# Eight gate slabs of a gated linear attention layer, moved into the scan as fp32 products

## The reference

```
p = h @ w_in                      # columns: q (512), k (512), v (1024), g (1024)
log_decay = log_sigmoid(low @ w_a2 + b_a) / 16          # per direction
for both directions, chunk by chunk (state is 128 x 256 for each of 4 heads):
    cum   = cumsum(log_decay)
    attn  = sum_d q[t,d] k[s,d] exp(cum[t,d] - cum[s,d])      # s before t
    out   = attn @ v + (q * exp(cum)) @ state
    state = exp(last) * state + (k * exp(last - cum))^T @ v
y = (rms_norm(out_forward + out_backward) * silu(g)) @ w_out
```

## Time and profile before

| | us |
|---|---|
| median of 3 runs | 1839.11 (1838.51 to 1839.13) |
| profiled execution | 1844.17 |
| its span on the core | 1842.4 |
| TensorE busy | 1687.5 (92%) |
| VectorE busy | 1166.0 (63%) |
| ScalarE busy | 727.2 (39%) |
| GpSimd busy | 110.0 (6%) |

### The profile page before, as it was taken

The page is one execution under the profiler, slowest core; times in us unless marked ns, Lnnn a source line. Parts: engine busy times, 40 slices in busy tenths (PEclk is TensorE's granted clock), DMA queues, the critical chain, the costliest instruction groups (busy, mean ns, idle before and its releaser), DMA issues.

```text
span 1842.4 us, 24024 instructions
## 1 busy us (share of the span) xinstructions
PE 1687.5 (92%) x8912; PEld 1436.4 (78%) x8912; DVE 1166.0 (63%) x1822; ACT 727.2 (39%) x1066; POOL 110.0 (6%) x70
## 2 busy tenths in 40 slices
PE   8999889987999999999997999976679799999996
PEld 6888777876888888888886778865567588888875
DVE  6688566469777577756855652158975665464465
ACT  3212555335342232322334562345533454343334
POOL 0200000123000000000012300000001200000002
PEclk9999999988999999999998899988879799999998
DMA  8334000131334333343221111200012123333221
GB/s 337 118 139 158 26 1 1 51 110 41 120 125 137 106 134 115 114 137 126 80 83 57 35 57 58 79 23 1 1 46 69 46 91 94 100 92 101 92 91 69
DMA packets 37278, 159.48 MB, mean 87 GB/s; under 512 B 4145, under 2 KB 4401, under 8 KB 31057
## 3 DMA queue, kind: packets, MB, share of 16 engines
q1 hardware_dynamic: 37202, 158.44, 25.7%
HBM read 156.33 MB, written 2.10 MB: 86 GB/s over the span
## 4 chain that ended last, share of the span: by engine, by line
PE 80%; DVE 11%; ACT 4%; issue 3%; DMA 1%; POOL 1%; SPq 0%; ACTq 0%; POOLq 0%; DVEq 0%
PE pm L402 63%; PE pm L422 5%; PE pm L594 4%; DVE row L1331 1%; DVE probs L1354 1%; PE pm L443 1%; DMA ada_w<-first_ada 1%; PE pm L717 1%; DVE h_res L1617 1%; ACT probs L878 1%; PE pm L530 1%; PE pm L470 1%; DVE o_r L1622 1%; PE pm L434 1%; PE pm L543 1%
## 5 line engine op out<-in xcount | busy, mean ns | idle before, releaser
L1180 DVE TENSOR_TENSOR w_lo<-raw,w_hi 128x1024 fp32r<-128x1024 f32 x193 | 243.2, 1261 | 425.7 <-ACT w_hi L807 423.4
L402 PE MATMUL pm<-x_hi,w_hi 128*128 128x512 f32 x1600 | 474.1, 356 | 14.0 <-DVE acc_g L1502 9.9
L402 PE MATMUL pm<-x_hi,w_lo 128*128 128x512 f32 x1600 | 473.5, 355 | 0.0
L402 PE MATMUL pm<-x_lo,w_hi 128*128 128x512 f32 x1600 | 470.7, 354 | 0.0
L807 ACT ACTIVATE w_hi<-raw 128x1024 fp32r<-128x1024 f32 x191 | 202.3, 1059 | 671.3 <-PE pm L402 616.0
L402 PEld LDWEIGHTS pm<-x_hi,w_hi 128*128 128x128 f32 x1600 | 262.9, 190 | 64.5 <-issue 15.6
L402 PEld LDWEIGHTS pm<-x_lo,w_hi 128*128 128x128 f32 x1600 | 261.0, 190 | 43.8
L402 PEld LDWEIGHTS pm<-x_hi,w_lo 128*128 128x128 f32 x1600 | 261.7, 190 | 42.8
L402 PE MATMUL pm<-hid_hi,w_hi 128*128 128x512 f32 (+1 forms) x396 | 119.6, 356 | 1.4 <-DVE w_lo L1180 1.4
L402 PE MATMUL pm<-hid_hi,w_lo 128*128 128x512 f32 (+1 forms) x396 | 120.6, 359 | 0.0
L402 PE MATMUL pm<-hid_lo,w_hi 128*128 128x512 f32 (+1 forms) x396 | 119.1, 355 | 0.0
(11 more groups left out here) (200 smaller groups left out, 2405.5 us busy)
## 6 DMA issues: line engine op xcount, KB each, us to landing
raw<-slabs SPq DMA_DIRECT2D x193, 512.0 KB, 3.5
ada_w<-ada SPq DMA_DIRECT2D x44, 1024.0 KB, 4.9
ada_w<-first_ada SPq DMA_DIRECT2D x4, 1024.0 KB, 18.8
h_res<-x SPq DMA_DIRECT2D x4, 768.0 KB, 16.9
out<-h_res SPq DMA_DIRECT2D x8, 256.0 KB, 2.0
rope<-rope SPq DMA_DIRECT2D x1, 512.0 KB, 23.4
level_f<-level SPq DMA_DIRECT2D x1, 448.0 KB, 4.2
vec<-vec SPq DMA_DIRECT2D x1, 272.5 KB, 2.8
```

The costliest lines, as they stand in the source:

```text
L402: last = pe.matmul(out_p[:, a:b], w[slot][:, ks], x[:, k, a:b], start=(k == 0 and w is w_hi and x is hi), stop=(k == tiles - 1 and w is w_lo))
L1180: dve.tensor_tensor(w_lo[nxt % 2][:, :], raw[nxt % 4][:, :], w_hi[nxt % 2][:, :].bitcast(FP32), ALU.subtract).then_inc(sem["split_lo"], 1)
```

## The change

The gate slabs leave the slab sequence (`slabs` has 185 instead of 193) and come as an input of their own, `gates`. They are not split. VectorE adds `x_hi` and `x_lo` back to fp32 for the 512 latent tokens (`join`, eight tiles `x_sum`, in the places of `w_hi` and `w_lo`). TensorE multiplies `gates` by `x_sum` in fp32, one product of 128x512 for each of the 8 x 8 tile pairs; they go in groups of three, three and two ahead of the level product in steps 0 to 23 of the 28. A half bank of `pm[2]` takes them, so the fifth turned key moves to `pm[1]` and the fifth state sum within `pm[2]`. ScalarE copies each gate slab out (`copy_gate`) and takes silu of two slabs once a head, behind the root (`open_gate`). SP loads gates into `raw[1]` and `raw[2]` in turn; the first two before the masks, the others behind them. The first two output slabs are loaded once gate products 7 and 8 are done, and split by ScalarE at b = 4 and VectorE at b = 5 and 6 of the last head, where before that was done in the gate stage. VectorE's masked copy of level b moves from step b to step b+1, behind `level_sides`; ScalarE's block copies likewise, level 6 to the start of the next head behind its first `level_decay`. The value loops of ScalarE and VectorE are unrolled. `sides0`, `sides1` and `o_lo2` change places in the memory of `x_hi` and `x_lo`.

```diff
@@ SP
+            def gate_load(i):
+                if i < 2:
+                    sp.wait_ge(sem["split_lo"], S_GLA_OUT - 3 + i)
+                else:
+                    sp.wait_ge(sem["gate_done"], i - 1)
+                sp.dma_start(gate_raw(i)[:, :], gates_in[i]).then_inc(gate_in[i % 2], 16)
+            gate_load(0)
+            gate_load(1)
             sp.wait_ge(sem["v_copied"], TOK // P + 8)
             sp.dma_start(level_f[:, :, :], level_in).then_inc(sem["level_in"], 16)
-            for u in range(3):
-                slab_load(4 * 29 + u, u)
+            for i in range(2, KT):
+                gate_load(i)
+            for u in range(2):
+                sp.wait_ge(sem["gate_done"], KT - 1 + u)
+                slab_load(S_GLA_OUT + u, 1 + u)
@@ TensorE
-            with pe.Fori(0, 2) as i:
-                for u in range(4):
-                    slab(S_GLA_G, i, u, x_hi, x_lo, LAT)
+            def gate_tiles(step_):
+                i = step_ // 3
+                if i >= KT:
+                    return
+                first = 3 * (step_ % 3)
+                if first == 0:
+                    pe.wait_ge(gate_in[i % 2], 16 * (i // 2 + 1))
+                    if i >= 1:
+                        pe.wait_ge(sem["gate_copied"], i)
+                for k in range(first, min(first + 3, KT)):
+                    pe.wait_ge(sem["x_sum"], k + 1)
+                    last = pe.matmul(gate_bank, gate_raw(i)[:, k * P:(k + 1) * P], x_sum[k][:, :],
+                                     start=(k == 0), stop=(k == KT - 1))
+                if first + 3 >= KT:
+                    last.then_inc(sem["gate_done"], 1)
             gram(0, 0)
             for h in range(GLA_HEADS):
                 for b in range(GLA_LEVELS):
+                    gate_tiles(GLA_LEVELS * h + b)
                     gram(h, b + 1)
@@ ScalarE
+            def copy_gate(step_):
+                i = step_ // 3 - 1
+                if step_ % 3 == 0 and 0 <= i < KT:
+                    act.wait_ge(sem["gate_done"], i + 1)
+                    act.activation(gla_g[:, i, :], gate_bank, ACT.Copy).then_inc(sem["gate_copied"], 1)
+            def open_gate(h):
+                act.wait_ge(sem["gate_copied"], 2 * h + 2)
+                act.activation(gla_g[:, 2 * h:2 * h + 2, :], gla_g[:, 2 * h:2 * h + 2, :], ACT.Silu).then_inc(
+                    sem["gate_open"], 1)
             for h in range(GLA_HEADS):
                 for b in range(GLA_LEVELS):
                     level_decay(GLA_LEVELS * h + b + 2)
+                    copy_gate(GLA_LEVELS * h + b)
                     if b == 0:
+                        if h >= 1:
+                            block_copy(h - 1, GLA_LEVELS - 1)
                         diagonal(h)
...
                     if h >= 1 and b == 5:
                         output_std(h - 1)
-                    if b >= BLOCK_LEVEL:
-                        block_copy(h, b)
+                        open_gate(h - 1)
+                    if h == GLA_HEADS - 1 and b == 4:
+                        for s in range(S_GLA_OUT, S_GLA_OUT + 2):
+                            act.wait_ge(sem["gate_done"], KT)
+                            split(s, s)
+                    if b > BLOCK_LEVEL:
+                        block_copy(h, b - 1)
                     if h >= 1 and b == 6:
                         finish_head(h - 1)
+            block_copy(GLA_HEADS - 1, GLA_LEVELS - 1)
             square_output(GLA_HEADS - 1)
+            open_gate(GLA_HEADS - 1)
             output_std(GLA_HEADS - 1)
@@ VectorE
+            def join(k):
+                dve.tensor_tensor(x_sum[k][:, :], x_hi[:, k, 0:LAT].bitcast(FP32), x_lo[:, k, 0:LAT].bitcast(FP32),
+                                  ALU.add).then_inc(sem["x_sum"], 1)
+            dve.wait_ge(sem["slab_done"], S_GLA_OUT - 1)
+            for k in range(KT // 2):
+                join(k)
+            dve.wait_ge(sem["slab_done"], S_GLA_OUT)
+            for k in range(KT // 2, KT):
+                join(k)
...
                     level_diff(m + 2)
                     level_sides(m + 1)
-                    if b < BLOCK_LEVEL:
-                        ... masked copy of level b
+                    if h == GLA_HEADS - 1 and b >= BLOCK_LEVEL:
+                        rest(S_GLA_OUT + b - BLOCK_LEVEL, S_GLA_OUT + b - BLOCK_LEVEL)
+                    if 1 <= b <= BLOCK_LEVEL:
+                        masked_copy(h, b - 1)
```

More of the change, by code:

```diff
@@ L47 @@
 S_GLA_V = S_GLA_Q + GLA_HEADS
-S_GLA_G = S_GLA_V + KT
-S_GLA_OUT = S_GLA_G + KT
+S_GLA_OUT = S_GLA_V + KT
 S_FFN1 = S_GLA_OUT + KT
@@ L93, in leave, with trunk @@
         self.n, self.extra = self.start + self.per * count, 0
-def trunk(nc, x_in, vec_in, rep_in, slabs_in, first_in, ada_in, rope_in, band_in, eye_in, a2_in, level_in, out):
+def trunk(nc, x_in, vec_in, rep_in, slabs_in, gates_in, first_in, ada_in, rope_in, band_in, eye_in, a2_in, level_in, out):
     ctx = ExitStack()
@@ L192, in trunk @@
         [chunk_sum, decay], _ = scratch(sums_at, ("chunk_sum", [2, GLA_HEADS, 6]), ("decay", [2, GLA_HEADS, 6]))
-        [o_hi2, o_lo2], at = scratch(x_at, ("o_hi2", [KT, LAT]), ("o_lo2", [KT, LAT]), dtype=FP32R)
-        [pairs, sides0, sides1, o_r], _ = scratch(
-            at, ("pairs", [2, LAT]), ("sides0", [2, LAT]), ("sides1", [2, LAT]), ("o_r", [LAT]))
+        [o_hi2], at = scratch(x_at, ("o_hi2", [KT, LAT]), dtype=FP32R)
+        [pairs, o_r], at = scratch(at, ("pairs", [2, LAT]), ("o_r", [LAT]))
+        assert at <= x_at + 4 * KT * TOK
+        [sides0, sides1], at = scratch(x_at + 4 * KT * TOK, ("sides0", [2, LAT]), ("sides1", [2, LAT]))
+        [o_lo2], at = scratch(at, ("o_lo2", [KT, LAT]), dtype=FP32R)
+        assert at <= hid_at
+        x_sum = [nc.alloc_sbuf_tensor_at(f"x_sum{k}", [P, LAT], FP32, offset=w_at + 4 * KT * P * (1, 3, 0, 2)[k // 2]
+                                         + 4 * LAT * (k % 2)) for k in range(KT)]
         pm = [ctx.enter_context(nc.psum_tensor(f"pm{j}", [P, 1024], FP32)) for j in range(4)]
@@ L216, in trunk @@
         ada_first = [ctx.enter_context(nc.semaphore(f"ada_first{j}")) for j in range(8)]
+        gate_in = [ctx.enter_context(nc.semaphore(f"gate_in{j}")) for j in range(2)]
         block = ctx.enter_context(nc.Block())
@@ L261, in state_sum, with turned_key, gate_raw @@
         def state_sum(j):
-            return (pm[1][:, 256 * j:256 * (j + 1)] if j < 4 else pm[2][:, TOK:TOK + 256])
+            return (pm[1][:, 256 * j:256 * (j + 1)] if j < 4 else pm[2][:, 0:256])
+        def turned_key(j):
+            return pm[2][:, j * P:(j + 1) * P] if j < 4 else pm[1][:, 0:P]
+        gate_bank = pm[2][:, LAT:2 * LAT]
+        def gate_raw(i):
+            return raw[1 + i % 2]
         def sides(m):
@@ L687, in turn_keys @@
                 for j, c in enumerate(SCAN[q % 2]):
-                    last = pe.transpose(pm[2][:, j * P:(j + 1) * P], k_out[:, c * P:(c + 1) * P], eye[:, :])
+                    last = pe.transpose(turned_key(j), k_out[:, c * P:(c + 1) * P], eye[:, :])
                 last.then_inc(sem["k_turned"], 1)
@@ L795, in split, with step @@
                 act.activation(w_hi[slot % 2][:, :], raw[slot % 4][:, :], ACT.Copy).then_inc(sem["split_hi"], 1)
-            def step(base, i, u, evacuate, first=False):
+            def step(base, i, u, evacuate, first=False, ahead=True):
                 s = base + u + 4 * i
@@ L804, in step @@
                 nxt = base + u + 2
-                if not (isinstance(s, int) and s + 2 >= N_SLABS):
+                if ahead and not (isinstance(s, int) and s + 2 >= N_SLABS):
                     act.wait_ge(raw_in[nxt % 4], 16 * (nxt // 4 + 1) + 16 * i)
@@ L1016, in _ @@
             act.wait_ge(sem["ld_done"], 2 * GLA_HEADS)
-            with act.Fori(0, 2) as i:
+            for i in range(2):
                 def take_value(s, i, u, src):
@@ L1029, in _ @@
                 for u in range(4):
-                    step(S_GLA_V, i, u, take_value)
+                    step(S_GLA_V, i, u, take_value, ahead=4 * i + u + 2 < KT)
                     if u >= 1:
@@ L1033, in _ @@
                 copy_value(3)
[L1035 to L1041, removed]
             INV = 1.0 / 16.0
@@ L1091, in diagonal @@
                 act.wait_ge(sem["gram_done"], n + 1)
+                if h == 0:
+                    act.wait_ge(sem["x_sum"], KT)
                 if h >= 1:
@@ L1181, in rest, with step @@
                                   ALU.subtract).then_inc(sem["split_lo"], 1)
-            def step(base, i, u, evacuate=None, first=False):
+            def step(base, i, u, evacuate=None, first=False, ahead=True):
                 s = base + u + 4 * i
@@ L1562, in _ @@
                     decays(n + 1)
[L1563 to L1568, removed]
+            for n in range(KT - 2):
+                step(S_GLA_V, n // 4, n % 4)
+            def join(k):
[7 more added lines that the diff above has]
+                join(k)
             dve.wait_ge(sem["psum_free"], S_GLA_OUT)
```

(13 more changed lines are left out.)

21 lines of the change are left out of this document (9 added, 12 removed).

## The result

| | before | after |
|---|---|---|
| median, us (10 runs each, one comparison) | 1839.92 | 1827.38 |
| ratio, 95% interval | | 0.9926 [0.9905, 0.9948] |
| span of the profiled execution | 1842.4 | 1826.3 |
| start of the scan, first `level_diff` | 1226.09 | 1181.35 |
| end of `scan(7)` | 1371.64 | 1355.67 |

One of the ten runs of the kernel after (1944.03 us, granted clock 0.828) was in a slower state of the chip; the ratio leaves it out, and the median of the other nine is 1826.63.

A forecast was written before the change was run, and what follows sets the result against it. TensorE was taken to bound the gate stage and VectorE the scan behind it. Scan start -43.0, schedule +7.5, clock +5.0 and other moved work +3.3 sum to -27.2: median 1811.9 us from 1839.11, range 1799 to 1829.

The forecast's parts named there:

- The start of the scan: First level_diff comes after the last value slab, at 1183.1 with the masks' transfer late: 43.0 us earlier.
- The groups are in TensorE's order, so I lay the three engines beside each other: In the scan, three engines' work laid out from head 1 to head 2: scan(4) ends at 41.9 for 38.6, +3.3.
- eight copies of 0.6: ScalarE's added gate slab copies, part of some 17 us in all, said to delay nobody.
- busy only 20 of 38.6: ScalarE's load in the scan before the change, in us, given as room for some 17 us of added work.
- the schedule: Engine layout of the scan at full clock: +2.6, +3.3 and +1.6 us between heads, nothing up to scan(0), sum +7.5.
- clock term: TensorE's dense row in the scan below full clock: 1.7 us for each of three heads, +5.0, ends 0 and 9.8.
- 1.6 more for the states: In the scan from head 1 to 2, VectorE loses 1.6 us waiting for TensorE's chunk states.
- the middle that I took: Clock between +3.3 us a head at 0.83 and nothing at full clock: 1.7 a head, since idle gaps invite a fall.
- The masked copies: In the scan, coming one level later saves at most the 5.7 us that they wait for TensorE.
- The moved work: VectorE in the last head: low parts of the first two output slabs, +2.5 us, and one masked copy more, +0.6.
- Rival 2: TensorE becomes the bound of the whole scan at its present clock: -11.4, 1827.7 us; chance 0.17.
- Rival 1: In the scan TensorE is never late, VectorE's own work covers the products: -43.0 + 3.3, 1799.4 us; chance 0.20.
- Rival 3: In the scan all 24 groups add their full length in a VectorE to TensorE loop: +15.3, 1854.4 us; chance 0.08.

The follow-up runs named there:

- e6_masks_early: e1_copy_first with the level masks loaded before the value slabs, ScalarE's decays and VectorE's cast made ahead too: ratio 0.9782 to the kernel before, 1799.45 us.
- e1_copy_first: Changed kernel with ScalarE copying the last gate slab out before its level decay instead of behind it: ratio 0.9821 to the kernel before, 1806.41 us.
- e5_copy_first_one: e1_copy_first with one product in each gate group instead of three or two, gates left incomplete: ratio 0.9800 to the kernel before, scan 152.4 us.
- e10_before_masks_later: Kernel before with only VectorE's masked copies and ScalarE's block copies one level later: ratio 0.9997, scan 144.7 us for 145.5.

## Why the prediction was right in sign and wrong in size

**The start of the scan** held: 43.8 us earlier for 43.0. The masks' transfer was the late one, as forecast (it took 3.2 us to land for the 4.2 of the earlier trace rows), and e6_masks_early got 4.1 us back by loading them early.

**The step that failed** is the one that begins "The groups are in TensorE's order, so I lay the three engines beside each other". I let every group start as soon as TensorE was free, and left out `pe.wait_ge(sem["gate_copied"], i)`, which stands in the diff ahead of each new slab. Its chain is VectorE's differences, decay, copy, products, level, next differences. I had even listed the copies ("eight copies of 0.6"), and priced them at nothing since ScalarE had the time ("busy only 20 of 38.6"); what counted was their place in ScalarE's order, behind the decay. Laid beside the schedule, from one end of `scan(2h)` to the next:

| stretch | before | forecast, without the clock term | e1_copy_first | after |
|---|---|---|---|---|
| scan start to `scan(0)` | 21.3 | 21.0 | 21.3 | 21.3 |
| `scan(0)` to `scan(2)` | 31.6 | 34.2 | 34.5 | 41.7 |
| `scan(2)` to `scan(4)` | 38.6 | 41.9 | 42.8 | 46.9 |
| `scan(4)` to `scan(6)` | 39.5 | 41.1 | 41.6 | 47.7 |
| `scan(6)` to `scan(7)` | 14.6 | 17.7 | 16.8 | 16.7 |

Without the wait the schedule is right to 0.9 us in each row. With it the three middle rows are 17.4 us longer. So the mechanism that I forecast (VectorE late at levels 1 to 3 and at the states, TensorE behind the blocks) is in the trace, with a second and larger one on top.

The rows agree better than their reasons do. I had VectorE's loss follow from the length of TensorE's row of pieces; but with 34 us less of products (e5_copy_first_one) only 4.6 us go, VectorE still waits 8.9 us for levels, and the "1.6 more for the states" stays as it is, three times 1.56. e10_before_masks_later has 2.7 us of that wait without any gate product in the scan, so at least a part of it comes with the moved copies. What the rest hangs on stays open.

**The clock term** was too large for the kernel that I had drawn up: with the wait gone (e1_copy_first) the three middle rows are 118.9 us for the 117.2 of the schedule, which, if the schedule is right otherwise, leaves 1.7 for it where I had 5.0. There the three stretches had a clock of 1.00, 0.96 and 0.92, against 0.88, 0.83 and 0.82 before:

```profile
1201.96:1236.47 34.51, 33.74 (x174) 23.82 (x175) 28.54 (x63) 16.82 (x33) 0.00 (x0) 1.00 0.10 32
1236.47:1279.27 42.80, 38.60 (x191) 26.84 (x189) 35.81 (x70) 24.16 (x41) 0.00 (x0) 0.96 0.08 25
1279.27:1320.85 41.58, 36.87 (x179) 26.02 (x178) 35.82 (x71) 23.68 (x40) 0.00 (x0) 0.92 0.12 39
```

The denser work kept the clock up: with the same order and one product in a group (e5_copy_first_one) the three stretches had 0.90, 0.83 and 0.83. That is what the Trainium skill says ("TensorE: Matmul & The Clock Gate", the part on the clock gate: throttled by default, released by sustained activity), and here the trace agrees with it more than with the middle that I took. In the changed kernel three groups ran for the most part at the low clock, 1.9 us more each, each behind an idle stretch of the wait (2.26, 2.67 and 3.74 us). So 5.7 us of TensorE's time did go to the clock there, about what I had set and in another place. The length of the idle stretch alone does not decide, since one of 2.63 us was followed by a group at full speed:

```profile
1252.77 2.81 PE L792 MATMUL pm<-x_sum,raw 128*128 128x512 f32 x6 [2.63 <-issue]
```

**The masked copies** were put right as a saving (at most 5.7 us, and alone it is 0.8 in the trace and nothing in the time), but the question was wrong. Their worth, with that of the block copies, is what they prevent once products stand ahead of the levels: 19 us.

**The moved work** of the last head, 3.1 us by the forecast, was 2.1 in the stretch to `scan(7)`.

**The rivals.** Rival 2 gave 1827.7, and 1827.38 was measured, but not for its reason: TensorE was busy 136.4 of the scan's 174.3 us and idle 16 us ahead of its own products, the clock of the scan was 0.92, and exchanging two instructions of ScalarE took 17.3 us away with every product still there. The agreement is an accident. Rival 1, a scan of 148.8, isn't reached even with one product in a group (152.4). Rival 3, the serial loop, was the right kind of mechanism at the wrong size: seven steps and not 24, and through the copy and not through the sides.

## What to carry to other kernels

When work is moved between the instructions of other stages, go through every wait that comes with it, and follow each to the place of its releaser in that engine's order: one operation of 0.58 us that had time to spare cost 17 us because it stood behind a decay that depends on the step itself, ahead of products that the step's level stands behind. An idle stretch that the profile puts down to "issue" and that comes once per buffer can be a wait for the buffer to come free, as here; look for the instruction that ended 0.1 us before, and move it to see. And a reordering that is worth nothing alone can be what another change rests on, so it is tried with it and not before it.

## What the runs showed of the hardware

TensorE's existing work ran faster because other work was put between it. From `scan(0)` to `scan(6)` TensorE was busy 74.0 us in the kernel before (the three windows of the earlier trace rows) and 109.2 in e1_copy_first (the three above), 35.2 more. The 53 gate products in that stretch are 45.6 us at 0.86 each. The 10.4 between, an estimate, is old work at the higher clock. With one product in a group (e5_copy_first_one) TensorE is busy 91.2 us there, of which 20 products are 17.2: the old work takes 74.0 again, at a clock of 0.90, 0.83 and 0.83.
